# The old states' transposes of a Mamba-2 scan, four blocks a group instead of eight

## What is computed

```python
states = einsum('bclgn,bcgel,bclgep->bcgepn', br, decay_states, xr)         # what these 8 tokens add
new_states = decay_chunk * h0 + states                                      # the state handed back
y_off  = einsum('bclgn,bcgepn,bcgel->bclgep', cr, states_in, exp(a_cs))     # what the old state h0 gives to y
```

## Time and profile before

| what | value |
|---|---|
| median of 3 executions | 2067.41 us (2067.36 to 2069.37) |
| the profiled execution, its own time | 2063.93 us |
| its span, first to last instruction | 2062.3 us |
| PE busy | 2007.0 us, 97% of the span |
| DVE, ACT, POOL busy | 1151.6, 937.7, 209.0 us |
| DMA | 373.29 MB, mean 181 GB/s |

### The profile page before, as it was taken

How to read it: one execution, slowest core, us unless ns; L and a number is a source line. 1 busy time by engine, 2 the same in 40 slices (tenths; PEclk the granted TensorE clock), 3 DMA queues, 4 the chain that set the end, 5 groups by cost and what they waited for, 6 DMA issues and landing times. The chain is left out here.

```text
span 2062.3 us, 40135 instructions
## 1 busy us (share of the span) xinstructions
PE 2007.0 (97%) x15826; PEld 1913.6 (93%) x15826; DVE 1151.6 (56%) x1832; ACT 937.7 (45%) x1533; POOL 209.0 (10%) x362
## 2 busy tenths in 40 slices
PE   6999999999999999999999999899999999999996
PEld 5899999999999999999999999899888888999996
DVE  5647766556465565456545543744554655565446
ACT  7535455325344253255433335534555555443443
POOL 1001000010110101000000000020234333200000
PEclk9999999999999999999999999999999999999998
DMA  9386555565665646755555566486789888765741
GB/s 249 113 243 178 143 144 141 133 184 137 165 170 128 184 131 169 207 148 150 145 148 156 143 180 229 123 266 183 209 270 269 264 249 253 223 194 158 246 152 64
DMA packets 539533, 373.29 MB, mean 181 GB/s; under 512 B 14907, under 2 KB 509688, under 8 KB 538474
## 3 DMA queue, kind: packets, MB, share of 16 engines
q1 hardware_dynamic: 519666, 306.53, 53.3%
q0 software_dynamic: 19680, 64.20, 10.1%
HBM read 349.48 MB, written 21.19 MB: 180 GB/s over the span
## 5 line engine op out<-in xcount | busy, mean ns | idle before, releaser
L123 ACT ACTIVATE w_high<-w_raw 128x2048 fp32r<-128x2048 f32 x232 | 443.6, 1912 | 627.6 <-PE bank L172 560.4
L128 DVE TENSOR_TENSOR w_low<-w_raw,w_high 128x2048 fp32r<-128x2048 f32 x232 | 530.8, 2289 | 219.5 <-ACT w_high L123 219.3
L167 PE MATMUL bank<-x_hi,w_high 128*128 128x320 f32 x1664 | 494.9, 312 | 0.0
L167 PE MATMUL bank<-x_lo,w_high 128*128 128x320 f32 x1664 | 489.5, 309 | 0.0
L167 PEld LDWEIGHTS bank<-x_hi,w_high 128*128 128x128 f32 x1664 | 312.3, 188 | 0.7
L167 PEld LDWEIGHTS bank<-x_lo,w_high 128*128 128x128 f32 x1664 | 312.6, 188 | 0.2
L172 PE MATMUL bank<-x_hi,w_low 128*128 128x320 f32 x1664 | 260.9, 309 | 0.0
L172 PEld LDWEIGHTS bank<-x_hi,w_low 128*128 128x128 f32 x1664 | 248.3, 188 | 0.0
L167 PE MATMUL bank<-xo_x_hi,w_high 128*128 128x320 f32 x640 | 198.0, 323 | 1.9 <-issue 1.6
L167 PE MATMUL bank<-xo_x_lo,w_high 128*128 128x320 f32 x640 | 188.9, 309 | 0.0
L2215 POOL DMA_DIRECT2D value_pages<-in_cache_v x232 | 124.9, 538 | 212.9 <-issue 134.8
(11 more groups left out here) (452 smaller groups left out, 3440.7 us busy)
## 6 DMA issues: line engine op xcount, KB each, us to landing
w_raw<-in_ev_w_in SPq DMA_DIRECT2D x104, 1024.0 KB, 5.7
w_raw<-in_od_w_in SPq DMA_DIRECT2D x40, 1024.0 KB, 6.8
w_raw<-in_ev_w_out SPq DMA_DIRECT2D x32, 1024.0 KB, 6.0
key_pages<-in_cache_k SPq DMA_DIRECT2D x256, 128.0 KB, 3.1
value_pages<-in_cache_v POOLq DMA_DIRECT2D x232, 128.0 KB, 3.5
w_raw<-in_ca_w_kv SPq DMA_DIRECT2D x16, 1024.0 KB, 7.0
w_raw<-in_ca_w_q SPq DMA_DIRECT2D x16, 1024.0 KB, 5.9
w_raw<-in_od_w_out SPq DMA_DIRECT2D x16, 1024.0 KB, 5.9
```

The lines of the kernel that those rows point to most:

```text
L123: self.nc.scalar.activation(self.w_high[n % HI][:], self.w_raw[n % RAW][:], ACT.Copy).then_inc(self.w_hi, 1)
L128: self.nc.vector.tensor_tensor(self.w_low[n % RAW][:], self.w_raw[n % RAW][:], self.w_high[n % HI][:].bitcast(F32), ALU.subtract).then_inc ...
L167: e.nc.tensor.matmul(out, hi[:, k, cols], rhs(k)[part], start=(k == 0 and part == 0), stop=False)
```

## The change

`Scan.steps` hands out the T steps in another order. Before, tiles o = 6 to 13 had one T each. Now o = 6, 8, 10 and 12 have two, and o = 7, 9, 11 and 13 have no step. N stays where it was, so in a tile with N both transposed states come ahead of it. All engines follow, since all read this list.

```diff
@@ Scan.steps
             if o == 6:
                 yield "B", g, 2
                 yield "P", g, 0
-            if 6 <= o < 14:
+            if o in (6, 8, 10, 12):
                 yield "T", g, o - 6
+                yield "T", g, o - 5
             if o in (8, 10, 12, 14):
                 yield "N", g, o // 2 - 4
```

## The result

The changed kernel takes 2074.91 us in the median of 7 executions (2071.84 to 2087.35), the kernel before 2068.58 us in the same number: 6.3 us between the medians. The ratio worked out from the single executions is 1.0043 with a 95% interval of 1.003 to 1.0056, or 6 to 12 us more. The forecast was 2069.5 us, no change; the time lies on the side of the rival with the slow stores, and just outside the range, which ended at 2074.8 us.

The account below looks back on a forecast made before the run. PE's own sequence at full clock was taken to bound the scan. Transposes 0, ACT's copies 0 and late loads 2.1 us were added to the median 2067.41 us, giving 2069.5 us, with a range of 2066.0 to 2074.8 us.

Parts of the forecast that it names:

- the rival with the slow stores: Second stores of pairs stay slow, so odd transposes wait: 7.4 us, 2074.8 us; 0.23 together with the own case's upper end.
- The sum: Over the whole kernel: 0 for transposes, 0 for ACT's copies, 2.1 us for loads needed a tile earlier.
- What bounds the kernel: In the scan, PE is busy 97% of the span at full clock, so its own sequence is the time.
- Part 1, the transposes: 0: On PE, 16 x 0.44 us leave odd tiles and 16 x 0.44 us join even ones: 0, within 0.3 us.
- Part 2, ACT's copies: 0: On ACT, the odd copy moves one tile earlier, covered by its waits for PE: costed at nothing.
- Part 3, the deadline and the lead: T (5) wants its state 17.71 us after N (0)'s block starts; stores lead weight loads by 0.44 us more, so are quick.
- Part 3, the landings: Second loads land 17.3 to 18.2 us after N's block starts, unchanged though the weights start 0.44 us later.
- the quick pairs: Five store and weight-load pairs in the kernel before: leads of 0.42 to 0.44 us, stores landing in 3.5 to 4.6 us.
- The upper bound: If weights land later by their whole delay, both places of a group could pay: 8 x 0.6 = 4.8 us at most.
- Part 3, the larger of two: Each group pays only the larger of its two holes, 0.42 us on average, plus 0.1 us for the semaphore.
- the stores don't move: On POOL behind N, stores keep their times while the weight load goes 0.44 us later, so every lead grows by 0.44 us.
- the first view: The profile page of the kernel before: PE busy 97% of the span, its clock granted in full throughout the scan.

Follow-up runs that it names:

- the stores first: The changed kernel with both stores of a pair issued ahead of both loads in POOL's queue: 2068.61 us, ratio 1.001 to the kernel before.
- the late pairs: The kernel before with only old states 4 to 7 of each group merged (o = 10 and 12): 2080.58 us, ratio 1.0066.
- the moved fetches: The changed kernel with a wait repeated 164 times at the start of PE's program, so instruction fetches fall elsewhere: 2073.47 us, ratio 1.0034.

## Why the prediction was wrong

The step that failed is the price of a late load. The sum priced a hole at its own length, and put the clock behind it at nothing without a reason; it also took the first stores of the pairs as fixed. Of the 11.0 us that the scan takes longer in the changed kernel's profile, the clock is 4.8, the one hole behind a delayed first store 2.9, and the holes that the sum was about 3.3, where it had 2.1. How the median's 6.3 us split is on no trace.

- *What bounds the kernel*: right for the kernel before. With the change PE's sequence is still the time, and the loss is PE's waits and the clock that falls behind them.
- *Part 1, the transposes: 0.* Right. S to T (4) is 17.27 or 17.28 us in every first place, and with the stores first the merged scan is within 0.3 us of the one before. An odd tile without a block gains nothing.
- *Part 2, ACT's copies: 0.* Right: no wait for `s0t` appears.
- *Part 3, the deadline and the lead.* Right in kind. T (5) and T (7) wait for the second load of their pair, the second stores are quick, as forecast, at seven of eight places (3.0 to 4.4 us in the first profile), and the late pairs alone turn them slow again. The rival with 2074.8 us came near the time by luck: its slow stores came back at one place of eight only.
- *Part 3, the landings.* A smaller miss: "the sum of bytes is the same, so I leave the landings where they are". In the four first places the weights landed at S + 17.2 to 17.9 (before: 16.6 to 17.5 at the quick pairs), about 0.3 us later, and the loads 0.7 us behind them as before, at S + 17.9 to 18.6. The upper bound had this, the sum didn't.
- *Part 3, the larger of two.* Another. A hole in the first place delays the second deadline, but also the end of tile o = 10 and with it the next weight load, on which the second landing hangs. So the second place pays again: 0.6 and 0.2 us in the first two groups of the first profile, 1.2 us in one of the second. Three profiles give 0.1 to 1.0 us, 0.55 us on average, at twelve first places, and 0 to 1.2 us at ten second places. In each of the three these holes come to 3.0 to 3.3 us, 1 us more than the 2.1 forecast and inside the bound of 4.8.
- *Part 3, "the stores don't move".* Failed in the last group. An instruction fetch lay on the first store behind N (1), which took 4.1 us in the one profile and 4.9 in the other; the second store fell behind the weights and became slow (6.1 and 6.3 us), and the holes were 2.9 and 6.5 us.
- *The sum, a hole at its own length.* Failed. The full clock of the first view belonged to a scan in which PE never waited. In the changed kernel's profile the clock adds 4.8 us to 6.2 us of holes.

## What to carry to other kernels

Before a step is pulled ahead, write down the landing of every transfer that it needs and the new deadline, and count the slack as spent when a competitor moves with the same edit. On an engine that is busy throughout, a hole costs more than its length when the clock falls behind it; here the waits went when the queue that feeds PE was reordered, both stores ahead of both loads. If moved work has no price where it stood, moving it has nothing to gain and can lose.

## What the hardware showed that I had not expected

- In the kernel before and the changed one, the second store of a pair (256 KB) took 3.0 to 4.6 us when it was issued 0.41 to 3.1 us ahead of a 1 MB weight load, and 5.7 to 6.7 us when its lead was 0.32 us or less, or when the weights went out just ahead of it. A 256 KB load issued behind the weights lands 0.7 us behind them, in the five quick pairs of the kernel before and the four first places of the changed one, and 3.0 to 3.3 us after its issue when they are held back.
- The Trainium skill, in "Runtime: NRT & Kernel Launch", section "Instruction fetch mechanics", calls the cost of a new 16 KB block of instructions mostly hidden. For PE the trace of the kernel before agrees: more than thirty such fetches fall into its scan, and PE has no hole there. But a store that a fetch meets pays: with the one at 825.25 it took 4.1 us against 2.7, and PE had a hole of 2.9 us behind it.
- In these traces no hole up to 0.63 us was followed by a drop of the clock. Of eight holes from 0.75 to 1.6 us (the changed kernel's two profiles, the late pairs, the moved fetches), four were, by 3.4 us at half clock. With each hole of 2.3 us or more came 6.8 to 17 us at half clock, some of it within the hole. Why some of the middle ones were spared stays open.
